# ScalarE and accumulating transfers take over the residual update in three feed-forwards

## The reference

```python
def swiglu(x, w_up, w_down):
    g, u = jnp.split(x @ w_up, 2, axis=-1)
    return (jax.nn.silu(g) * u) @ w_down

n = rmsnorm(h, P['norm_g'][l, 0]) * (1 + sc0) + s0
h = h + 0.5 * g0 * swiglu(n, P['w_ffn_up'][l, 0], P['w_ffn_down'][l, 0])
```

## Time and profile before

| what | value |
|---|---|
| median of 3 runs | 3137.64 us (3137.29 to 3138.24) |
| the profiled execution | 3137.54 us, of which its trace spans 3135.4 us |
| TensorE busy | 3018.9 us, 96% |
| VectorE, ScalarE, GpSimd busy | 68%, 36%, 3% |
| mean granted TensorE clock | 0.982 |

### The profile page before, as it was taken

The page is one execution under the profiler, slowest core; times in us unless marked ns, Lnnn a source line. Parts: engine busy times, 40 slices in busy tenths (PEclk is TensorE's granted clock), DMA queues, the critical chain, the costliest instruction groups (busy, mean ns, idle before and its releaser), DMA issues.

```text
span 3135.4 us, 48664 instructions
## 1 busy us (share of the span) xinstructions
PE 3018.9 (96%) x19892; PEld 2938.2 (94%) x19892; DVE 2122.9 (68%) x3521; ACT 1141.8 (36%) x1820; POOL 85.8 (3%) x164
## 2 busy tenths in 40 slices
PE   7999999998999999999999999999899999999998
PEld 4899999997899999999999999999789999999998
DVE  7666666646655557988968988863565556785675
ACT  3422312422444433434343433442154443443432
POOL 0000000000000000000000000000000000000000
PEclk8999999999999999999999999999999999999999
DMA  8255553345122532444322434334521242122222
GB/s 304 91 202 228 213 190 135 115 153 221 67 75 85 192 112 80 135 141 142 122 95 94 149 121 142 108 114 163 224 82 71 76 186 108 68 95 81 95 68 75
DMA packets 89743, 408.90 MB, mean 130 GB/s; under 512 B 10049, under 2 KB 13569, under 8 KB 68914
## 3 DMA queue, kind: packets, MB, share of 16 engines
q1 hardware_dynamic: 60384, 285.76, 25.6%
q0 software_dynamic: 19872, 94.53, 8.3%
q10 hardware_dynamic: 9266, 25.50, 2.2%
HBM read 359.46 MB, written 46.30 MB: 129 GB/s over the span
## 4 chain that ended last, share of the span: by engine, by line
PE 77%; DVE 14%; ACT 4%; issue 3%; DMA 1%; ACTq 0%; DVEq 0%
PE tile_psum L743 21%; PE misc_psum L860 12%; PE tile_psum L750 11%; PE misc_psum L864 6%; PE tile_psum L1215 6%; PE tile_psum L704 3%; PE tile_psum L1219 3%; PE misc_psum L669 3%; PE tile_psum L669 2%; PE tile_psum L860 2%; PE tile_psum L709 2%; PE tile_psum L1080 1%; DVE h L2254 1%; DVE wlo L2083 1%; PE tile_psum L864 1%
## 5 line engine op out<-in xcount | busy, mean ns | idle before, releaser
L743 PE MATMUL tile_psum<-n_hi,whi 128*128 128x320 f32 x1536 | 352.3, 311 | 4.0 <-issue 2.2
L743 PE MATMUL tile_psum<-n_lo,whi 128*128 128x320 f32 x1536 | 350.1, 309 | 0.0
L2083 DVE TENSOR_TENSOR wlo<-raw,whi 128x2048 fp32r<-128x2048 f32 (+4 forms) x130 | 250.6, 1930 | 114.2 <-ACT whi L1491 112.2
L743 PE MATMUL tile_psum<-x_hi,whi 128*128 128x320 f32 x1300 | 300.1, 312 | 17.4 <-DVE h L2254 11.7
L743 PE MATMUL tile_psum<-x_lo,whi 128*128 128x320 f32 x1300 | 298.3, 311 | 0.0
L743 PEld LDWEIGHTS tile_psum<-n_hi,whi 128*128 128x128 f32 x1536 | 257.6, 189 | 6.8 <-DVE n_lo L2174 4.2
L743 PEld LDWEIGHTS tile_psum<-n_lo,whi 128*128 128x128 f32 x1536 | 258.2, 189 | 0.0
L1491 ACT ACTIVATE whi<-raw 128x2048 fp32r<-128x2048 f32 (+4 forms) x130 | 208.9, 1616 | 126.7 <-DMA raw<-in_w_down 43.7
L1215 PE MATMUL tile_psum<-n_hi,whi 128*128 128x320 f32 x768 | 237.4, 320 | 11.0 <-ACT gate_out L1978 10.3
L2254 DVE SCALAR_TENSOR_TENSOR h<-tile_psum,ada_t,h 128x320 f32<-128x320 f32 (+2 forms) x408 | 154.2, 434 | 129.2 <-PE tile_psum L750 127.5
L750 PE MATMUL tile_psum<-n_hi,wlo 128*128 128x320 f32 x1536 | 241.3, 309 | 0.0
(11 more groups left out here) (384 smaller groups left out, 6450.1 us busy)
## 6 DMA issues: line engine op xcount, KB each, us to landing
w_ada<-in_w_ada POOLq DMA_DIRECT2D x72, 512.0 KB, 4.0
raw<-in_w_up SPq DMA_DIRECT2D x72, 512.0 KB, 3.8
raw<-in_w_up SPq DMA_DIRECT2D x34, 1024.0 KB, 4.9
w_ada<-in_w_ada SPq DMA_DIRECT2D x56, 512.0 KB, 6.3
raw<-in_w_gate SPq DMA_DIRECT2D x24, 1024.0 KB, 4.9
raw<-in_w_down SPq DMA_DIRECT2D x29, 768.0 KB, 4.4
whi<-table_keep SPq DMA_DIRECT2D x20, 1024.0 KB, 4.7
wlo<-table_keep SPq DMA_DIRECT2D x20, 1024.0 KB, 6.9
```

The costliest lines, as they stand in the source:

```text
L743: pe.matmul(tps[:, t.s, m, 0:TH], blk(p, m * n + k)[0], (hi, lo)[b][:, k, tok], start=k == 0 and b == 0, stop=False)
L2083: ins = dve.tensor_tensor(lo_at(r, n)[:, 0:w], raw_at(r, n)[:, 0:w], hi_at(h_, n)[:, 0:w].bitcast(F32), ALU.subtract)
```

## The change

In chunks 0, 1 and 2 of the three fast feed-forwards VectorE no longer updates h. ScalarE copies each down tile out of PSUM with the gate as its scale into one of two halves of `hf` (j = 0 or 1), frees the tile and raises `h_staged`. GpSimd waits for that and issues a transfer from `hf` to `h` with an accumulating add (`h_added[j]`). ScalarE waits before it stages (i + 1, j) until the transfer of (i, j) has landed, and once more in `keep_p5` before `hf` is used again. GpSimd waits for all landings at the start of chunks 1 and 2, VectorE before chunk 3's down stage. GpSimd's `w_ada` loads are spread over the steps in which VectorE uses such tiles. ScalarE's four `fast_group` calls are spread between the stagings.

```diff
+            def add_to_h(i, j):
+
+                tok = slice(j * TH, (j + 1) * TH)
+                pool.wait_ge(h_staged, due(h_staged))
+                pool.dma_start(h[:, 2 * i:2 * i + 2, tok], hf[:, :, tok], accum_op=ALU.add).then_inc(h_added[j], 16)
+                due(h_added[j], 16)
+
+            def fast_ffn(l, f):
+
+                plan = ADA_PLAN[l, f]
+                for c, n in enumerate(FAST_CHUNKS):
+                    if 0 < c < 3:
+                        for each in h_added:
+                            pool.wait_ge(each, due.now(each))
+                    for q in range(n):
+                        ada_loads(plan[q])
+                    for i in range(4):
+                        if c < 3:
+                            add_to_h(i, 0)
+                        ada_loads(plan[n + i])
+                        if c < 3:
+                            add_to_h(i, 1)
+                    plan = plan[n + 4:]
...
-                        for t in range(ADA_LATE, DEPTH * ADA_TILES):
-                            pool.wait_ge(ada_used, t - 1)
-                            pool.dma_start(adaw[:, t % 2, :], w_ada[t]).then_inc(ada_late[t % 2], 16)
+                        ada_loads(2)
+                        fast_ffn(0, 1)
+                        fast_ffn(1, 0)
+                    else:
+                        fast_ffn(1, 1)
...
+            def stage_h(l, section, i, j):
+
+                t = tile()
+                if i:
+                    act.wait_ge(h_added[j], due.now(h_added[j]))
+                for m in range(2):
+                    for a, b, g in HALVES[j]:
+                        ins = act.activation(hf[:, m, a:b], tps[:, t.s, m, a - j * TH:b - j * TH], ACT.Copy,
+                                             scale=ada[:, l * ADA_TILES + 8 * section + 2 * i + m, g:g + 1])
+                ins.then_inc(t.free, 1)
+                act.wait_ge(t.free, t.free_at)
+                act.sem_inc(h_staged, 1)
+                due(h_added[j], 16)
...
             def keep_p5(g):
+                if g % 6 == 0:
+                    for each in h_added:
+                        act.wait_ge(each, due.now(each))
...
                     for i, j in walk(4):
-                        slots.tile()
                         if j == 0 and i < 2:
                             round_panel()
                         elif j == 0 and i == 2:
                             at[0] += 6
-                            for k in range(4):
-                                fast_group(fast[0], k)
+                            fast_group(fast[0], 0)
+                        elif i == 2:
+                            fast_group(fast[0], 1)
                         if c == 0 and (i, j) in ((0, 0), (0, 1)):
                             sum_to_hi(1 if j == 0 else 3)
+                        stage_h(l, section, i, j)
+                        if (i, j) == (2, 1):
+                            fast_group(fast[0], 2)
+                        elif (i, j) == (3, 0):
+                            fast_group(fast[0], 3)
...
                     if c == 3:
+                        for each in h_added:
+                            dve.wait_ge(each, due(each, 16 * 12))
                         return into_h_last(section, plan[n:], *last)
                     junk_at[0] = junk_down
                     for i, j in walk(4):
-                        update(section, i, j)
+                        t = slots.tile()
                         if j:
                             continue
+                        if c == 0 and i == 0:
+                            seen(t)
```

More of the change, by code:

```diff
@@ L520, in program @@
         ada_late = [sem(f"ada_late_in{k}") for k in range(2)]
+        h_staged, h_added = sem("h_parts_staged"), [sem(f"h_parts_added{j}") for j in range(2)]
         ada_in, ada_used = [sem(f"ada_in{k}") for k in range(2)], sem("ada_used")
@@ L1431, in _, with ada_loads @@
             pool.dma_start(sm_keep[1], sml[:, :].bitcast(F32)).then_inc(small_kept, 16)
+            late = [ADA_LATE]
+            def ada_loads(n):
+                for _ in range(n):
+                    t = late[0]
+                    if t == DEPTH * ADA_TILES:
+                        return
+                    late[0] += 1
+                    pool.wait_ge(ada_used, t - 1)
+                    pool.dma_start(adaw[:, t % 2, :], w_ada[t]).then_inc(ada_late[t % 2], 16)
+            def add_to_h(i, j):
[18 more added lines that the diff above has]
+                    plan = plan[n + 4:]
             for p, kind in enumerate(KINDS):
@@ L1696, in sum_to_hi, with fast_ffn @@
                 act.activation(sum_hi[i], sum_raw[i], ACT.Copy).then_inc(n_sum_hi, 1)
-            def fast_ffn(norm, last, before_last):
+            def fast_ffn(l, section, norm, last, before_last):
                 for c, n in enumerate(FAST_CHUNKS):
@@ L1825, in _ @@
                 if l:
-                    fast_ffn((l, 0), (l, 1), before_mixer)
+                    fast_ffn(l, 2, (l, 0), (l, 1), before_mixer)
                 else:
@@ L2063, in _ @@
                 into_h_last(l, 2)
-                fast_ffn((l, 2), (l + 1, 0), lambda: None)
+                fast_ffn(l, 8, (l, 2), (l + 1, 0), lambda: None)
             act.wait_ge(c_kept, 16)
```

## The result

The change makes the kernel slower. Medians: 3146.79 us after (seven runs, 3141.89 to 3150.92) against 3138.07 before (seven runs, 3136.32 to 3141.39); the ratio is 1.0031, 95% interval 1.0022 to 1.0040. The forecast was 3122.0 with a range of 3117 to 3144. The profiled execution took 3144.66 us.

What follows compares the result with a forecast made beforehand. TensorE, busy 96%, was taken to lose 26.5 us in down stages; less 9.0 for the first gap and 0.9 left in place gives 16.6, less 1.0 for new waits 15.6: 3137.6 to 3122.0 us, range 3117 to 3144.

Steps and rivals of the forecast that it cites:

- L: Time of a 320 KB accumulating transfer from issue to landing, taken as 4.3 us; no profile row had one.
- What bounds the kernel, and what is removed: Down stages of chunks 0 to 2: TensorE waits on VectorE's update of h; removing 216 updates gives 16.6 us.
- ScalarE's copies: Staging from PSUM in chunks 0 to 2: 76 us in all, hidden, a tile freed some 1.2 us after it's done.
- The 0.9 us left at (0, 1) of the third chunk 0: Third feed-forward: ScalarE first rounds the late fourth sum of n, so 0.9 of that stage's 1.4 us loss stays.
- The issue: GpSimd issuing the 72 adds: 0.53 us each, costing it nothing.
- The engines' share: DMA traffic in the down stages: called light, at a share of 0.13 to 0.43.
- Wait (a): Staging (i+1, j) waits for landing (i, j): hidden by two tiles, 7.0 us in chunk 0, 10.6 in the others.
- Wait (b): GpSimd's queue: the add of (i, 1) stands behind an ada load; in chunk 0 (2, 1) goes out 4.7 us late.
- (c): Next fast stage: keep_p5 waits for every landing, keep_u2 behind it; L may be 6.4, after chunk 0 4.4; charged 1.0.
- The first rival: Slow landings delay fast stages: L of 6.4 to 7.6, 3132 to 3144 us, chance 0.09; slower, up to 3223, 0.13.
- the second: L of 5 to 6.4, two transitions lose: 3124 to 3131 us, still faster; chance 0.18 together with a moved stall.
- The first gap: Chunk 0 of the first two feed-forwards: 2.86 us wait ending with VectorE's hidden; 4.5 us each with clock, left in place.

Runs made afterwards that it cites:

- first_copy: The changed kernel with plain copies in place of accumulating adds, both transfers of an i ahead of its ada loads: 3121.65 us, 0.9955 to the kernel before.
- plain_copy: The changed kernel with transfers that don't accumulate, GpSimd's queue order kept: 3129.66 us, 0.9973 to the kernel before.
- four_halves: The changed kernel with both adds ahead of the ada loads and, in the third feed-forward alone, even i staged in gate_act's buffer: 3134.13 us, 0.9991 to the kernel before.
- adds_first: The changed kernel with both adds of an i ahead of its ada loads in GpSimd's program: 3139.01 us, 1.0005 to the kernel before.
- c12_first_plan: Change in chunks 1 and 2 alone, adds ahead of ada loads, chunk 0's ada tiles moved to those chunks' down stages (3, 2, 2, 2): 3123.82 us, 0.9954.
- c12_first: The change in chunks 1 and 2 alone, both adds of an i ahead of its ada loads: 3135.04 us, 0.9994 to the kernel before.
- plan2_only: The kernel before with chunk 0's ada tiles moved to the down stages of chunks 1 and 2 (3, 3, 2, 1), no transfers: 3149.17 us, 1.0047.
- c12_first_plan3: Change in chunks 1 and 2 alone, adds first, ada tiles 2, 2, 2, 2 in their down stages, two left in chunk 0: 3118.03 us, 0.9945.
- the plans 3, 3, 2, 1: Four kernels, with and without transfers, with ada tiles 3, 3, 2, 1 in down stages of chunks 1 and 2: 3142.28, 3154.28, 3149.17, 3145.66 us.

## Why the prediction was wrong

The step that failed is the cost of the transfers: one L of 4.3 us for all 72, on the sentences that DMA traffic is light in these stages and that 72 more issues cost GpSimd nothing. L was right only in the quiet stages (4.0 to 4.8). In chunk 0 and at its end it rose to 9.5, and behind chunks 1 and 2 the adds that `keep_p5` waits for took 6.4 to 6.8, just past the 6.4 that the prediction allowed them. The miss is 24.8 us. Adds in place of copies make some 16 of it, and the order of GpSimd's queue, charged at 1.0 together with the wait of `keep_p5`, makes some 8.

- **What bounds the kernel, and what is removed.** Right. The waits on the update are gone, and the stages of chunks 1 and 2 lose nothing. first_copy takes 14.1 us off, of the 15.6 forecast, though with the adds' order mended as well.
- **ScalarE's copies.** Hidden by themselves. They take 521, 422 and 369 ns, where the rows of the same forms gave 442, 327 and 284, so 94 us by the same sum and not 76. Four pieces in a row still span 1.23 us. The 0.9 us left at (0, 1) of the third chunk 0 came: TensorE waited 0.84. But (0, 1) isn't the only place where ScalarE is late. At (0, 0) it also has a panel and a sum to round first, and there it staged that tile 3.1 us after TensorE was done with it, not 1.2.
- **The issue.** 1.20 us against 0.53. The same transfer as a copy takes 0.71 (plain_copy), and the add makes the rest. Why the copy takes more than a w_ada load isn't shown.
- **The engines' share.** The forecast read shares of 0.33 to 0.43 in chunk 0 as room. An add holds the engines 2.3 times as long as a copy, and a load that had 4.0 us took 4.7. In the second chunk 0 stage the share went from 0.42 to 0.77. The Trainium skill ("Collectives: The Full Stack", Part 3, why ReduceScatter is half of AllGather) says that an add there needs two source reads where a copy needs one, for rings between cores; that is 2 times the reads. The runs show 2.3 times the engines' time for an add within one core's SBUF, so they bear it out roughly. The prediction used it for L alone, not for the time on the engines.
- **Wait (a)** was called hidden by two tiles. In the third feed-forward the first add lands after 9.5 us against 7.0 of cover, and the stage lost 3.9 us more than before; four_halves takes just that away. TensorE's wait there was 2.5 us, and by the row above 1.9 of it is the late staging of (0, 0) (an estimate: 3.1 less 1.2), so a longer L alone would have cost less.
- **Wait (b)** was seen: the add of (2, 1) goes out 5.1 us after the tile (forecast 4.7). It was charged only in chunk 0, at 1.0 us together with (c). By adds_first the order costs some 8 us, and most of what the traces show of it lies behind chunks 1 and 2. VectorE was ahead there, as the prediction said. What it left out is that the add then follows an ada load of 512 KB within 0.7 to 0.8 us, shares the engines with it, and lands after 6.4 to 6.8 us and not 4.2 to 4.8.
- **Wait (c).** Forecast: u2 is kept at 6.0 + 2L + 0.9 from tile (2, 1), with L of 4.4 as the edge. Measured from 1270.0, `keep_u2` ends at 1290.6, 20.6 us after and not 15.5: two landings of 6.2 and 6.8 us where 4.3 stood twice, which is 4.4 of the 5.1. The formula held, its L didn't.
- **The rivals.** What happened lies between the first and the second: landings of up to 9.5 us in chunk 0, where they meet (a) as well, and of 6.4 to 6.8 at four of the six transitions behind chunks 1 and 2. The first rival's limit of 6.4 held: TensorE began to wait there, and these four fast stages lost 0.5 to 0.9 us each. But it had one L for every transition and needed over 7 us in all of them. A rival with L apart for quiet and crowded places was missing.
- **The first gap** stayed, as said. It isn't fixed, though: without the ada tiles ahead of it, it goes (c12_first_plan).

The sum by the runs: the forecast 3122.0 is about what first_copy gives, 3121.65 measured and 3123.9 by its ratio. Adds in place of copies in that order cost 0.5% (0.9955 to 1.0005), some 16 us, all of it in the chunk 0 stages and the fast stages behind them. The queue's order costs another 8. That gives 3146, the kernel after. That an ada load ahead of an add makes its landing long, adds_first shows. That weight loads do it in chunk 0 is only argued: three of them go out within 1 us of the first add of the third feed-forward's chunk 0, but no run moved them. Also open is the longer gap in c12_first's chunk 0.

## What to carry to other kernels

Price a transfer at the place where it counts: ask which loads go out with it or just ahead of it, and how long each holds the engines, before calling a share of 0.4 room. When an operation that nobody waited for becomes one that somebody waits for, look at how many buffers lie between, and at what stands ahead of it in its in-order queue; two lines of order gave 8 us here. And look for work that can leave the crowded stage before changing who does the work in it. VectorE's ada tiles were the real load of chunk 0: without them the stage takes 29.6 us on VectorE's own update (plan2_only). Moving most of them to chunks 1 and 2, with the transfers in those two chunks alone, won 17.8 us (c12_first_plan3), where staging chunk 0 itself lost.

## What the runs showed of the hardware

- A 320 KB accumulating transfer from SBUF to SBUF lands 4.1 us after its issue in the quiet chunk 1 of the third feed-forward, where a copy of the same shape lands in 2.7, and holds the DMA engines 2.3 times as long (2,480 against 1,090 us for 72).
- Issued 0.7 us behind a 512 KB load of the same queue such an add landed after 6.8 us, issued 0.7 us ahead of it after 4.3. The engines' share was 0.92 and 0.95 meanwhile.
- GpSimd takes 1.20 us to issue it, 0.88 at half the size, 0.71 as a copy and 0.56 for a plain load.
- The kernel before spreads over 5 us in the seven runs beside the result and over 18 us in the eighteen beside the plans 3, 3, 2, 1. A difference of a few us between groups is no evidence without the ratios.
